# A two-layer mixer and expert step on one core: the first expert's rows gathered in two halves, the late states as row quarters, and a few moves around the first experts

## The reference

```python
for l in range(DEPTH):                       # DEPTH = 2
    h = rmsnorm(x) @ w_in                    # u | q | k | v | g
    x += concat(pool_mix(u), gate(g) * groupnorm(retention(q, k, v, state))) @ w_out
    # new_state = state * decay + k'^T v     (samples: 8 sequences x 4 heads x 128 x 128)
    h = rmsnorm(x)
    g = argmax(h @ w_rg); experts = top2 of the 4 experts in group g
    for e in range(16):
        x += gate_e * (silu(h @ w_gate[e]) * (h @ w_up[e])) @ w_down[e]
y = rmsnorm(x)
```

## Time and profile before

| | |
|---|---|
| median of 3 runs | 810.65 us (810.26 to 810.99) |
| the profiled execution | 810.1 us, its span 808.3 us, mean granted PE clock 0.996 |
| PE busy | 792.4 us (98%) |
| DVE busy | 601.0 us (74%) |
| ACT, POOL busy | 478.4 us, 331.7 us |
| first gather of layer 0, of layer 1 | issued at 231.95, 628.45 us |
| experts of layer 0 | about 236 to 387 us |

### The profile page before, as it was taken

One profiled execution on the slowest core, in us unless ns is written; L12 is line 12 of the kernel. 1 busy time (PEld: TensorE's weight loads), 2 busy tenths in 40 slices (PEclk: granted clock), 3 DMA queues, 4 the chain that ended last, 5 costly groups with the idle time before them and its releaser, 6 DMA issues.

```text
span 808.3 us, 11933 instructions
## 1 busy us (share of the span) xinstructions
PE 792.4 (98%) x4092; PEld 628.5 (78%) x4092; DVE 601.0 (74%) x951; ACT 478.4 (59%) x816; POOL 331.7 (41%) x225
## 2 busy tenths in 40 slices
PE   9999999999999999999999999999999999999995
PEld 6887788878757888888588787888776678888861
DVE  5445655575789999999754456646658899999986
ACT  5633333612578888887663432444335798888874
POOL 0015996310042355664100199925012234656530
PEclk9999999999999999999999999999999999999998
DMA  8832223224959999998753322222379699999967
GB/s 295 288 117 66 78 66 118 105 79 150 409 187 386 375 362 377 398 370 296 273 187 104 86 73 71 66 80 91 99 296 346 240 416 347 387 377 396 342 226 287
DMA packets 57295, 188.17 MB, mean 233 GB/s; under 512 B 10862, under 2 KB 11886, under 8 KB 49036
## 3 DMA queue, kind: packets, MB, share of 16 engines
q1 hardware_dynamic: 44476, 156.56, 53.7%
q0 software_dynamic: 10368, 23.09, 7.7%
q10 hardware_dynamic: 2400, 7.87, 2.6%
HBM read 172.99 MB, written 29.39 MB: 250 GB/s over the span
## 4 chain that ended last, share of the span: by engine, by line
PE 55%; DVE 29%; issue 8%; DMA 6%; ACT 2%; DVEq 0%; SPq 0%; POOL 0%; ACTq 0%; POOLq 0%
PE ps L499 13%; PE ps L503 10%; PE ps L502 10%; DVE gul L2198 9%; DVE dnl L2203 7%; DVE hgTl L2214 4%; PE ps L501 3%; DMA back<-y_d 2%; PE ps L1483 2%; PE ps L1485 2%; PE ps L1484 2%; DVE y L2223 2%; DMA y_d<-y,rowidx 2%; PE ps L1462 2%; DVE act L2235 1%
## 5 line engine op out<-in xcount | busy, mean ns | idle before, releaser
L911 POOL DMA_INDIRECT y_d<-y,rowidx x32 | 118.2, 3695 | 121.6 <-DVE y L2223 114.5
L499 PE MATMUL ps<-wh,hT 128*128 128x512 f32 x408 | 163.5, 401 | 0.2
L2198 DVE TENSOR_TENSOR gul<-wgu,eh 128x1024 fp32r<-128x1024 f32 x128 | 150.7, 1222 | 0.1
L2189 DVE SCALAR_TENSOR_TENSOR wl<-raw,gcol,wh 128x512 fp32r<-128x512 f32 x80 | 78.5, 983 | 75.8 <-ACT wh L1133 75.7
L1164 ACT ACTIVATE eh<-wgu 128x1024 fp32r<-128x1024 f32 x128 | 128.5, 1057 | 4.0 <-PE ps L1485 3.9
L503 PE MATMUL ps<-wh,lT 128*128 128x512 f32 x313 | 122.4, 391 | 0.0
L502 PE MATMUL ps<-wl,hT 128*128 128x512 f32 x313 | 121.9, 390 | 0.0
L1483 PE MATMUL ps<-eh,hgTh 128*128 128x512 f32 x240 | 96.6, 402 | 0.4 <-issue 0.4
L1485 PE MATMUL ps<-eh,hgTl 128*128 128x512 f32 x240 | 93.8, 391 | 0.0
L1484 PE MATMUL ps<-gul,hgTh 128*128 128x512 f32 x240 | 93.5, 389 | 0.0
L1133 ACT ACTIVATE wh<-raw,gcol 128x512 fp32r<-128x512 f32 x80 | 57.3, 719 | 60.3 <-PE ps L501 56.2
(11 more groups left out here) (277 smaller groups left out, 1612.6 us busy)
## 6 DMA issues: line engine op xcount, KB each, us to landing
wgu<-in_gate_up SPq DMA_DIRECT2D x64, 1024.0 KB, 12.3
wdn<-in_w_down SPq DMA_DIRECT2D x64, 512.0 KB, 14.3
raw<-in_w_in SPq DMA_DIRECT2D x79, 256.0 KB, 2.7
raw<-in_w_out SPq DMA_DIRECT2D x32, 256.0 KB, 3.0
back<-y_d SPq DMA_DIRECT2D x16, 512.0 KB, 6.1
s<-in_state_ret POOLq DMA_DIRECT2D x8, 512.0 KB, 4.1
xn_d<-xf ACTq DMA_DIRECT2D x8, 512.0 KB, 7.6
x_in<-in_x_cols SPq DMA_DIRECT2D x8, 288.0 KB, 4.9
```

What stands on the lines that cost most here:

```text
L499: pe.matmul(out, both, w_h, start=first, stop=False)
L911: pool.indirect_dma_start(out=y_d, out_offset=bass.IndirectOffsetOnAxis(ap=rowidx[:, 1, e:e + 1], axis=0), in_=y[s][:, :], in_offset=None, ...
L2189: ve.scalar_tensor_tensor(out=wl[S % SPL][:, :], in0=raw[S % RAW][:, :], scalar=gcol[:, 0, L, s % KC:s % KC + 1], in1=wh[S % SPL][:, :].bi ...
L2198: ve.tensor_tensor(gu_pair(gul, gul3, e, s, p), gu_pair(wgu, wgu3, e, s, p), gu_split(e, p)[:, :].bitcast(F32), ALU.subtract).then_inc(glo, 1)
```

## The change

Six things are changed, in both layers.

1. Expert 0's rows come in two gathers of 512 columns each (`gather_half`), by row numbers of their own (`halfidx` = 2 x row + half, in the table seen as rows of 512). `halfidx` is written ahead of `rowidx` and `tidx_done` counts both. PE waits for the left half (`gat_left`), turns it over and multiplies blocks 0 and 1; then it waits for the right half (`gat[0]`) and turns that over. The gathers of experts 1 and 2 follow the two.
2. The late states: `kd_late` holds both heads' keys under one another (64 rows each) and `v_late` holds v for four sequences at a time, so that each of the four products has 32 rows of its own. `late_new` issues the four behind one another at the end, with one `skv_mm`. Two of the `late_old` go to where the first `late_new` stood. 11 idle products follow instead of 1.
3. SP issues three of the four loads of expert 3 ahead of the stores of the late states, and the last one behind expert 6's gate and up weights.
4. DVE's first two splits of expert 0's weights go ahead of the wait for the softmax terms.
5. ACT's switch to the Silu table goes from behind the softmax terms to behind the first two splits of expert 1's weights; its late states are in another order.
6. In expert 0's turn, `rows_hi` and `rows_lo` of the first half of expert 1's rows go ahead of the third split of expert 1's weights.

```diff
+            def gather_half(e, half, sem):
+                cols = slice(512 * half, 512 * half + 512)
+                pool.indirect_dma_start(out=hg[e % 3][:, cols], out_offset=None, in_=xn_d.rearrange("r (h d) -> (r h) d", h=2),
+                                        in_offset=bass.IndirectOffsetOnAxis(ap=halfidx[:, half:half + 1], axis=0),
+                                        bounds_check=half_bound, oob_is_err=False).then_inc(sem, 16)
...
                 pool.wait_ge(xn_st, 16 * NT * (L + 1))
-                pool.wait_ge(tidx_done, L + 1)
-                for e in range(3):
+                pool.wait_ge(tidx_done, 2 * L + 1)
+                gather_half(0, 0, gat_left)
+                gather_half(0, 1, gat[0])
+                pool.wait_ge(tidx_done, 2 * L + 2)
+                for e in (1, 2):
                     gather(e)
...
             ve.wait_ge(tab_mm, L + 1)
+            for half in range(2):
+                last = ve.tensor_scalar(halfidx[:, half:half + 1], ps[2][:, 0:1], 2.0, 2.0 * NO_ROW + half, ALU.mult, ALU.add)
+            last.then_inc(tidx_done, 1)
...
-            ve.wait_ge(exp_out, 2 * L + 2)
+            gu_lo(L, 0, 0, range(2))
+            ve.wait_ge(by_act, 3 * L + 3)
...
-            gu_lo(L, 0, 0, range(3))
+            gu_lo(L, 0, 0, (2,))
...
+            def late_new(L):
+                pe.wait_ge(vb_done, 3 * L + 1)
+                for h in range(2):
+                    for n in range(2):
+                        rows = slice(NSAMP * h + 32 * n, NSAMP * h + 32 * n + 32)
+                        last = pe.matmul(ps[B_LATE[h][n]][:, :], kd_late[rows, :], v_late[rows, :, :], start=False, stop=True)
+                last.then_inc(skv_mm, 1)
...
-                for h, n in LATE_STEPS[1:]:
-                    late_old(L, h, n)
-                    late_new(L, h, n)
-                idle_turns(3, 1)
-                pe.wait_ge(gat[0], 16 * used(L, 0, 0))
-                rows_t(0, t_mm, pair=True)
+                late_old(L, *LATE_STEPS[3])
+                late_new(L)
+                idle_turns(3, 11)
+                pe.wait_ge(gat_left, 16 * (L + 1))
+                rows_t(0, t_mm, pair=True, halves=(0,))
...
                     if first(e) and k == 2:
+                        pe.wait_ge(gat[0], 16 * used(L, 0, 0))
+                        rows_t(0, t_mm, halves=(1,))
                         pe.wait_ge(hg_hi, rows_split(L, e, 0))
...
                 sp.wait_ge(gat[0], 16 * used(L, 0, 0))
+                sp.wait_ge(skv_mm, 3 * L + 1)
+                load_gu(L, AHEAD, 0)
+                load_dn(L, AHEAD, 0, ks=(0,))
                 for j in (1, 0):
-                    sp.wait_ge(s_late, 4 * L + (4, 3)[j])
+                    sp.wait_ge(s_late, 4 * L + (4, 2)[j])
                     sp.dma_start(o["new_ret_sample"][L, LATE + j], s_out[j][:, :, :]).then_inc(late_st, 16)
                 for s in range(3):
                     sp.wait_ge(gat[s], 16 * used(L, s, 0))
+                load_gu(L, 6, 0, after=0)
                 sp.wait_ge(late_st, 64 * (L + 1))
-                load_gu(L, AHEAD, 0)
-                load_dn(L, AHEAD, 0)
-                load_gu(L, 6, 0, after=0)
+                load_dn(L, AHEAD, 0, ks=(1,))
...
                 late_state(L, 3, 0)
                 sc.wait_ge(most_done, L + 1)
-                table(ACT.Silu)
                 late_state(L, 3, 1)
+                late_state(L, 2, 0)
                 late_state(L, 2, 1)
                 rows_hi(L, 0)
                 gu_hi(L, 1, 1, 0, range(2))
+                table(ACT.Silu)
                 experts(sc, lambda e, s, n: expert(L, e, s, n))
...
                 if not final(e):
-                    gu_lo(L, e + 1, (s + 1) % 3, range(ahead_of_act))
+                    gu_lo(L, e + 1, (s + 1) % 3, range(2))
+                if first(e):
+                    rows_lo(L, 1, (0,))
+                    gu_lo(L, 1, 1, (2,))
```

More of the change, by code:

```diff
@@ L206, in build @@
         rowidx = tile("rowidx", [P, 2, NE], U32)
+        halfidx = tile("halfidx", [P, 2], U32)
         tab = region + 4096 * 3
@@ L313, in build @@
         on = [heads_tile(f"on{t}", d_at + 2048 * t if t < LAST else r12 + 10 * 1024) for t in range(NT)]
-        vb = [tile(f"vb{i}", [P, DECB, P], off=(d_at, d_at + 4096, gn_at, d_at + 4096)[i]) for i in range(NH)]
+        vb = [tile(f"vb{i}", [P, DECB, P], off=d_at + 4096 * i) for i in range(LATE)]
+        v_late = tile("v_late", [P, 4, P], off=gn_at + 2048)
         gu3_at, dn3_at = (s0_at[0], d_at), (gn_at, region + 4096 * 8)
@@ L338, in build @@
         gu3_ld = [sem(f"gu3_ld{h}") for h in range(2)]; dn3_ld = [sem(f"dn3_ld{k}") for k in range(2)]
-        gat = [sem(f"gat{i}") for i in range(3)]
+        gat = [sem(f"gat{i}") for i in range(3)]; gat_left = sem("gat_left")
         early_ld = [sem("early_ld0"), sem("early_ld1")]
@@ L652, in load_gu, with load_dn @@
                     sp.dma_start(dst, a["gate_up"][L, e, :, 4 * h:4 * h + 4, :]).then_inc(ld, 16)
-            def load_dn(L, e, s, after=None):
-                for k in range(2):
+            def load_dn(L, e, s, after=None, ks=range(2)):
+                for k in ks:
                     if after is not None:
@@ L1485, in three, with rows_t @@
                 return pe.matmul(out, lo_l, hi_r, start=False, stop=final)
-            def rows_t(s, sem, pair=False):
-                for half in range(2):
+            def rows_t(s, sem, pair=False, halves=range(2)):
+                for half in halves:
                     for k in range(4):
@@ L2203, in dn_lo, with rows_lo @@
                     ve.tensor_tensor(dn_chunk(dnl, dnl3, e, s, k), dn_chunk(wdn, wdn3, e, s, k), dn_split(e, k)[:, :].bitcast(F32), ALU.subtract).then_inc(dlo, 1)
-            def rows_lo(L, e):
-                for half in range(2):
+            def rows_lo(L, e, halves=range(2)):
+                for half in halves:
                     ks = slice(4 * half, 4 * half + 4)
@@ L2238, in expert @@
                 else:
-                    rows_lo(L, e + 1)
+                    rows_lo(L, e + 1, (1,) if first(e) else range(2))
                     gu_lo(L, e + 1, (s + 1) % 3, range(ahead_of_act, 4))
```

61 lines of the change are left out of this document (31 added, 30 removed).

## The result

The changed kernel is slower: 815.42 us, the median of 17 runs (811.73 to 818.84), against 810.98 us (17 runs, 809.46 to 813.5) of the kernel before in the same sessions. The ratio is 1.0049, with a 95% interval of 1.0037 to 1.0061. Measured once more, later, it was 1.0048 (1.0029 to 1.0068). The prediction said 810.1 us and no change.

A forecast was written before the change was run, and what follows sets the result against it. PE and DVE were taken as full in the experts, so only their start could move: 0.6 - 0.3 = 0.3 us a layer, twice, from the median 810.65 to 810.05, told as 810.1 us; range 808.6 to 812.0.

The forecast's parts named there:

- its length does not change by a move inside it: Experts' loop: PE and DVE are busy throughout, so its length is fixed and only its start can move.
- SyncE's queue: Expert 3's loads leave at about 237.2, not 242.46; no engine waited for a weight load, so gain 0, cost 0.
- Every us by which the products of expert 0 start earlier is a us of the total: Start of the experts: an earlier or later start counts in full in the total, once in each of two layers.
- The sign that the prediction itself had named: Experts' stretches: the forecast is wrong if one of them is not full in one of the two kernels.
- Start of the pipe: Expert 0's gather in halves: the left half lands 0.6 us earlier than the whole, between 0 and 1.2 us.
- rival B: Expert 0's gather: bytes decide, the left half lands 1.2 us earlier, total 808.9; chance 0.18.
- The cover for the right half: Expert 0's second half gather: it lands 0.5 us before PE asks for it; later landing would cost in full.
- Late states, tables, idle products: Ahead of expert 0: four row-quarter products take 1.1 us, idle products and ACT's table switch fit; cost 0 to 0.1 us.
- rival D: Late states: row quarters run one after another, transposes start 1.05 us later, total 813.4; chance 0.06.
- Expert 1's low rows: DVE in expert 0's turn: low rows ahead of a weight split leave the same work for DVE and PE; 0.
- 2 x 0.3: Total gain over two layers: each saves 0.6 us by the half gather and loses 0.3 us to PE's split, 0.6 us less.
- Rival E: Expert 1's rows: their gather lands late among the weight loads and PE waits, 812.6 to 818; chance 0.07.

The follow-up runs named there:

- last_load_later: Changed kernel with SyncE's wait for the stores and expert 3's last down load moved behind expert 5's loads: 819.78 us, ratio 1.0092.
- gathers_first: Changed kernel with SyncE's waits for all three gathers ahead of expert 3's early loads: 817.62 us, ratio 1.0062.
- no_gather_wait: Changed kernel without SyncE's waits for the gathers of all three slots behind the stores: 815.42 us, ratio 1.0047.
- only_queue: Kernel before with SyncE's new load and store order alone: 811.09 us, ratio 0.9999.
- old_order: Changed kernel with ACT's table load, expert 1's rows and the first weight remainders where they were before: 817.89 us, ratio 1.0083.
- whole_gather: Changed kernel with expert 0's rows in one gather, PE's wait and transposes to match: 810.31 us, ratio 1.0000.
- state_and_order: Changed kernel with expert 0's rows in one gather and SyncE's old queue: 810.91 us, ratio 1.0003.
- only_halves: Kernel before with the two half gathers alone: 812.25 us, ratio 1.0014.
- halves_layer0: Changed kernel with the half gathers in the first layer alone, the second fetching expert 0's rows whole: 812.57 us, ratio 1.0019.
- halves_layer1: Changed kernel with the half gathers in the second layer alone: 812.97 us, ratio 1.0018.
- late_gathers: Changed kernel with one whole gather for expert 0 and two fills on GpSimd delaying the gathers of experts 1 and 2: 811.78 us, ratio 1.0002.
- gu4_first: Changed kernel with expert 4's gate and up loads ahead of SyncE's wait for the stores: 816.54 us, ratio 1.0063.
- halves_together: Changed kernel with PE waiting for both half gathers before the first transposes: 816.23 us, ratio 1.0056.
- stores_first: Changed kernel with the two stores issued ahead of expert 3's three early loads: 811.78 us, ratio 1.0014.
- changed_again: The changed kernel itself, unedited, measured once more beside the kernel before: 815.22 us, ratio 1.0048.

## Why the prediction was wrong

**The step that failed** is the first one: "its length does not change by a move inside it. What can change is the time at which the pipe starts", and with it, of SyncE's queue, "No engine waited for a weight load" and "Cost 0". The lack of a wait was read as room, and the room was never measured. It was 0.7 us for expert 5's second load, and the load landed 2.8 us later. "Every us by which the products of expert 0 start earlier is a us of the total" failed with it: 1.00 us was won ahead of expert 0, and 1.28 and 1.13 us were lost in experts 0 to 5, 0.65 us between the layers and 3.64 us behind the last expert, where the prediction had no term at all. The transfers of the stretch from 236 to 272 us run at a mean of 372 GB/s before, with the DMA engines busy at a share of 1.01 to 1.03 in each 4 us from 248 us on. last_load_later and gathers_first show what lateness costs there: one load issued 4.2 us later, and expert 3's loads 4.7 us later, gave 12 us of waits each. The half gathers were counted as what they do to PE's start (the saving) and to PE's order (the split), and not as one more transfer in a stretch that is full of them. The sign that the prediction itself had named, a stretch of the experts that is not full, came true.

**Start of the pipe: right in kind, too small.** The left half took 3.43 us to land in layer 0, and in layer 1 the transposes began 3.46 us after its issue (629.53, 632.99), so it saves 4.36 - 3.43 = 0.93 us, not 0.6. That lies between the forecast and rival B's 1.2.

```profile
231.42 3.43 DMA hg<-xn_d,halfidx
```

(This is the chain of no_gather_wait, whose gathers are the changed kernel's; in the latter the issue at 231.62 and the transposes at 235.09 are 3.47 us apart.) The Trainium skill (DMA: Bandwidth & Descriptors, Anatomy of one DMA — SWDGE (gpsimd) path) would have had 0.34 us for it, by the estimate in the prediction. Here the measurement decides: 0.93. The cover for the right half was there in layer 0 and not in layer 1, where the chain goes through it. There GpSimd's issue of the second half took 2.02 us, where it was 1.35 in layer 0:

```profile
630.94 4.64 DMA hg<-xn_d,halfidx
635.63 0.66 PE ps L1510 x4
```

**Late states, tables, idle products: right.** The four row quarters took 1.14 us against my 1.1, so rival D did not come. The Trainium skill's figure (TensorE: Matmul & The Clock Gate, Part 3: Packing small matmuls — row/col tiling) gave 3.5 / 3.07 = 1.1 us as an estimate; the trace agrees.

**SyncE's queue: right alone, by only_queue.** Its new order is worth 0.9999. Beside the halves it is not free of effect: with the stores first the changed kernel falls from 1.0049 to 1.0014.

**Expert 1's low rows:** old_order gives no gain from undoing it; alone it was not measured.

**The loop of the experts** was taken as fixed. In whole_gather, state_and_order and only_halves it takes 93.67 us for ten experts, not 93.17, which is 0.05 us an expert and 1.0 us in both layers. It eats most of what the start gained there: -0.74 at the start of layer 0 and -0.45 between the layers. So "2 x 0.3" would not have been seen in the total even without the halves. Why an expert takes 9.37 us and not 9.32 is open: PE and DVE are busy throughout in both (85.00 of 85.00 us from 290 to 375 us).

**The rivals.** Rival E named the right side and a price that holds the measured time (812.6 to 818), but not the mechanism: there is no idle of PE ahead of expert 1's rows, as the stretch of expert 0 shows (columns as in the earlier trace rows):

```profile
236.40:247.20 10.80, 10.80 (x56) 8.93 (x55) 9.37 (x13) 8.19 (x12) 3.41 (x3) 1.00 0.93 313
```

The time was lost at experts 4 and 5 and behind expert 15. That its price holds the measured time is luck. (Its lower price should read 812.1: 2.0 us on top of the forecast, as its 818 is reckoned.)

**What stays open.** Shown is that the half gathers cause the loss (whole_gather; only_halves alone is at the edge of the noise), that each layer makes its own (halves_layer0, halves_layer1), and that it appears as late weights of experts 4 and 5 and as a longer end, which a lower clock lengthens further. Not shown is the link from the one to the other. It is not the later issue of the other gathers (late_gathers), nor SyncE's wait for them (no_gather_wait), nor the place of expert 4's load (gu4_first). The earlier need is a part: the waits go when the experts start late (halves_together). But it is the smaller part, 1.0 us against the 2.8 us by which expert 5's second load landed later; in no_gather_wait that load landed 2.6 us later too (issued at 258.86, 20.66 us), and in only_queue 0.5 us (259.95, 17.4 us), within the 0.7 us to spare. Why the halves make it later is open. The earlier need alone does not fit stores_first, with the earliest start but one in the table and waits of 0.4 us, unless the stores' place brings the bytes forward; they were indeed ahead there, 9.38 MB by 264 us against 8.46 MB:

```profile
q1 hardware_dynamic: 1650, 9.38, 82.3%
```

The bytes alone are not the answer either: late_gathers had moved 8.39 MB by then, less than the changed kernel, and waited 2.2 us.

For the late rows at the end (2.87 of the 3.64 us) no experiment has a cause. Two versions would have told more and were not run: one with an unused gather of the same size beside a whole one, and halves_together with idle products in TensorE's wait.

## What to carry to other kernels

An engine that never waits for a load does not show that the load has time to spare: read how full the transfers are in the stretch ahead of its use, and price how late it may come before the start of its consumer is moved forward. A transfer that is split to start sooner should be tested alone and together with each of the other edits: here the halves cost 0.14% alone and 0.49% with the rest, and dropping them while placing the stores first made the only version that beat both. When the runs of a kernel spread over 7 us, a single trace shows a run and not the kernel. Where an experiment makes TensorE wait, read the granted clock behind the wait before the time is put down to the wait.

## What the runs showed of the hardware

The half gathers added almost no packets. Queue q0 of the changed kernel and of the kernel before (packets, MB, share), both over the whole span:

```profile
q0 software_dynamic: 10400, 23.09, 7.7%
```

```profile
q0 software_dynamic: 10368, 23.09, 7.7%
```

Thirty-two more for two more gathers, so 16 each, and the same bytes; 31 of the 32 are under 512 B by the two pages. So the halves added no data packets: a half row did not make smaller packets than a whole one. Gathers whose descriptors go out behind queued loads land late: in late_gathers, with expert 3's loads issued from 236.05 and the last of the three gathers from 236.22, SyncE waited for them until 246.9, some 9.6 us behind the end of that issue (237.31). In gathers_first, with nothing in front of it, the last of them (issued at 235.53 for 1.56 us) had landed by 241.4, so 4.3 us behind the end of its issue. And a store of 512 KB that is queued behind 2.5 MB of loads and another store completed about 14 us after its issue (240.47 to 254.60), with 8.9 us of SyncE's time behind it in only_queue, at no cost to the total.

TensorE's granted clock fell to 0.50 behind idle stretches of 3.17 us (changed kernel, 784.85), 3.02 and 3.88 us (changed_again) and 1.85 and 1.96 us (halves_together), and stayed at 1.00 behind one of 2.13 us (gathers_first, up to 386.19), so the length of the last idle stretch alone did not decide it here.
